# A weighted sum of gathered rows with the rows as moving operand, another order of places for the first gathers, and early scores for a second head

## The chip, the cores and the metric

The kernel runs on one core of a Trainium2 chip. The metric is the device time of one execution in microseconds. TensorE (PE) does the matrix products, VectorE (DVE), ScalarE (ACT) and GpSimd (POOL) the element-wise work; SyncE (SP) and GpSimd issue transfers, which run on sixteen DMA engines.

## The reference

Two blocks follow each other on x of 256 tokens by 1024. The change lies in the last part of the first block, the expert layer `peer_ffn`; the rest (a modulated norm, one input projection, sparse attention, a short convolution, an output projection; then two layers of window attention and spatial gating) is not touched. In short form, for each token:

```python
mod = silu(c) @ w_ada + b_ada          # six parts of 1024; gate2 is the last
h2  = rms_norm(x, norm2_w) * (1 + scale2) + shift2
q   = (h2 @ peer_wq).reshape(8 heads, 2 halves, 128)
s   = einsum(q, peer_subkeys)          # 8 heads x 2 halves x 128 keys
vals, idx = top_k(s, 16)               # in each half
top_s, pos = top_k(all 256 sums of a value of either half, 16)
expert = idx0[pos // 16] * 128 + idx1[pos % 16]
g = softmax(top_s)
a = gelu(dot(peer_u[expert], h2))      # 16 experts for each token and head
y = sum over heads and experts of g * a * peer_v[expert]
x = x + gate2 * y
```

Each of 256 tokens picks 16 experts in each of 8 heads. All is fp32.

## The kernel before

The 256 tokens are two tiles of 128, a token to a partition. A group g (0 to 15) is one head of one tile: groups 0 to 7 are the heads of tile 0, 8 to 15 those of tile 1. A group has 16 picks; pick n = 16 g + j is expert j of each of its 128 tokens. The table `peer_uv` holds a row of u and its row of v side by side, 2048 numbers or 8 KB, so one gather (GpSimd's indirect DMA at L898) brings 128 rows, 1 MB, and there are 256 gathers. They go to twelve places, six in `rows` (places 0 to 5) and six in `low_pairs` (6 to 11); pick n takes place n % 12 (`pair`, L438). All gathers stand in one queue in order, and GpSimd, which issues them in order, waits before gather n for `pair_used`, the count of picks that TensorE has summed, to show that pick n - 12 is done.

At the start some places hold something else. Places 0 to 5 lie on `flat`: places 2 and 3 are the query weights of heads 0 and 1, place 4 their keys, place 5 holds `cbc`, the silu of c in all partitions. Places 8 to 11 are `last_ada`, the eight tiles of w_ada that make gate2. Before gathers 2 and 3 GpSimd waits for TensorE's queries of head 0 and 1, before gather 4 for the scores of both, before gather 5 (`LAST_ADA_SLOT`) for all eight modulation tiles (L886 to L901).

**Routing** (`route`, L2050, on VectorE): the top 16 of each half, the top 16 of the sums, and the experts' numbers; `routed` lets GpSimd issue that group's gathers. Scores come from TensorE: `score_query(h)` makes the queries of both tiles at once (L1545), `score_keys(h)` the scores (L1558), and ACT copies both out (L1100, L1106). Head 0 of tile 0 is made ahead of that by `early_scores_of_head_0` (L1570 to L1585), so that `route(0)` starts as soon as the first tile's h2 is there. VectorE then does `route(0)`, the eight modulation tiles (`last_ada_tiles`, L1764: a product of two SBUF operands with a running sum), `route(1)`, and after that the loop over groups, in which `route(g + 2)` is cut into three parts between the dots.

**The loop over groups.** For each pick VectorE multiplies the u half of the row with h2 and sums (`dot`, L2061; h2 by token lies in PSUM). After four picks ACT makes the gelu (L1137), VectorE the weight g * a (L2068), and ACT four diagonal matrices `diag`, the identity scaled by each token's weight (L1142). TensorE then adds the v halves (`sum_pair`, L1566): for each of eight chunks of 128 columns it loads that chunk of the rows as weights and streams the diagonal matrix through, which gives the weighted rows turned, features on partitions, added up in PSUM over the 128 picks of a tile. In the profile an fp32 matmul is two records, each with a weight load of its own; so a pick is 16 records. The last group is cut finer (4, 2, 2 and then single picks), and TensorE, ACT and VectorE start the next block's first projection (`vg`) among its picks (L1609 to L1611 are its products). `join` (L2077) adds gate2 times the sum to xT, straight from PSUM. It stands after group 9 for tile 0 and at the end for tile 1; for tile 1, ACT and VectorE then split xT into a high and a low part (L1131, L2075), on which the second tile of `vg` waits.

**Order.** Each engine's order is written out by hand in its block; waits are on counting semaphores. SP loads weights in its own order; after the picks it waits for pick 253 to land before its second load of the next block, and for pick 255 before the third (L842, with L808's row loads between).

## Time and profile before

| | |
|---|---|
| median of 3 runs | 1178.29 us (1177.71 to 1179.69) |
| profiled execution | 1180.36 us |
| its span on the core | 1178.4 us, mean granted clock 0.972 |
| PE busy (matmul records) | 1051.1 us, 89%, 7587 |
| DVE busy | 837.5 us, 71% |
| ACT busy | 433.0 us, 37% |
| POOL busy | 268.8 us, 23% |
| q0, the gathers' queue | 268.45 MB, 55.0% of 16 engines |
| q1, SP's queue | 120.10 MB, 27.8% |
| q8, instructions | 60 packets, 0.98 MB, 0.3% |

All times in the profile are microseconds from the start of the span. PE is TensorE's matmuls, PEld its weight loads, which run beside them. A timeline line gives start, duration, engine, source line, operation, the tile written and those read, the shapes, the number of instructions merged into the line and, in brackets, how long the engine stood idle before and what ended that. In the views by window each engine's busy time stands with the number of instructions that ended in it, then the share of TensorE's clock that was granted, the mean busy share of the sixteen DMA engines, and GB/s.

### The profile page before, as it was taken

Reading aid. Unit: us, or ns where it says so; the run is one execution under the profiler, and the core shown is the slowest. Engines: PE = TensorE matmul, PEld = TensorE weight load, DVE = VectorE, ACT = ScalarE, POOL = GpSimd, SP = SyncE. Lnnn points to the kernel's source line nnn. Section 1 sums busy time; section 2 is a strip of 40 time slices with the busy share of each in tenths; the row PEclk is TensorE's granted clock in tenths of the full one; section 3 lists DMA queues with packets and bytes.
Section 4 is the critical chain, followed back from the end, with each engine's and each line's share of the span. In section 5 each row is a group of like instructions: output and inputs, shape, how many; then the busy total and the mean of one; then the engine's idle time right before and its main releaser. Section 6 shows DMA issues by size and latency. Waiting matters only on the chain.

```text
span 1178.4 us, 18884 instructions
## 1 busy us (share of the span) xinstructions
PE 1051.1 (89%) x7587; PEld 980.2 (83%) x7587; DVE 837.5 (71%) x1801; ACT 433.0 (37%) x913; POOL 268.8 (23%) x289
## 2 busy tenths in 40 slices
PE   8999987999999987777877778878999999999997
PEld 6999986998899877777877777778899888898886
DVE  7978889667667667666776766655756868765776
ACT  3635832123212221222122122211557654476452
POOL 1000005343334333333333333434000000300000
PEclk9999999999999999998999999989999999999999
DMA  9965988999999999999999999999854655455540
GB/s 371 406 244 180 348 313 307 420 421 420 421 420 420 421 420 421 420 421 420 420 420 421 420 421 422 420 422 420 325 208 161 237 205 184 147 211 179 186 171 36
DMA packets 59480, 390.35 MB, mean 331 GB/s; under 512 B 6785, under 2 KB 7809, under 8 KB 15618
## 3 DMA queue, kind: packets, MB, share of 16 engines
q0 software_dynamic: 36864, 268.45, 55.0%
q1 hardware_dynamic: 21056, 120.10, 27.8%
q8 instruction: 60, 0.98, 0.3%
q10 hardware_dynamic: 1474, 0.60, 0.2%
q14 instruction: 26, 0.21, 0.0%
HBM read 388.08 MB, written 1.05 MB: 330 GB/s over the span
## 4 chain that ended last, share of the span: by engine, by line
PE 63%; DMA 24%; DVE 6%; ACT 4%; issue 1%; SPq 0%; another core or an unknown queue 0%; DVEq 0%; ACTq 0%
DMA rows<-in_peer_uv,work 23%; PE aux L1566 23%; PE pj L1609 6%; PE pj L1611 5%; PE pj L1610 5%; PE aux L1545 5%; PE pj L1286 5%; PE pj L1287 4%; PE pj L1288 4%; DVE rows L2061 2%; DMA rows<-in_w_ada 1%; PE aux L1360 1%; ACT work L1142 1%; ACT rows L1010 1%; PE aux L1425 1%
## 5 line engine op out<-in xcount | busy, mean ns | idle before, releaser
L1566 PE MATMUL aux<-work,rows 128*128 128x128 f32 x2080 | 263.4, 291 | 73.8 <-ACT work L1142 73.8
L1566 PEld LDWEIGHTS aux<-work,rows 128*128 128x128 f32 x2080 | 256.2, 206 | 81.6 <-ACT work L1142 81.4
L1566 PE MATMUL aux<-work,low_pairs 128*128 128x128 f32 x2016 | 238.2, 279 | 30.2 <-ACT work L1142 30.1
L1566 PEld LDWEIGHTS aux<-work,low_pairs 128*128 128x128 f32 x2016 | 233.0, 195 | 34.0 <-ACT work L1142 34.0
L898 POOL DMA_INDIRECT rows<-in_peer_uv,work x130 | 125.5, 965 | 301.2 <-PE aux L1566 232.1
L707 DVE TENSOR_TENSOR wlo<-wring,whi 128x1024 fp32r<-128x1024 f32 x100 | 121.0, 1235 | 77.6 <-ACT whi L701 77.1
L898 POOL DMA_INDIRECT low_pairs<-in_peer_uv,work x126 | 118.3, 939 | 158.5 <-PE aux L1566 153.4
L1286 PE MATMUL pj<-xh,whi 128*128 128x256 f32 x512 | 146.3, 286 | 0.4
L1137 ACT ACTIVATE work<-work 128x4 f32<-128x4 f32 (+2 forms) x71 | 14.7, 207 | 358.3 <-DVE work L2061 358.3
L1287 PE MATMUL pj<-xl,whi 128*128 128x256 f32 x512 | 144.8, 283 | 0.0
L1288 PE MATMUL pj<-xh,wlo 128*128 128x256 f32 x512 | 144.8, 283 | 0.0
L2061 DVE CUSTOM_DVE_ANT_0 low_pairs<-low_pairs,aux 128x1024 f32<-128x1024 f32 x64 | 77.6, 1220 | 53.9 <-DMA low_pairs<-in_peer_uv,work 53.9
L701 ACT CAST whi<-wring 128x1024 fp32r<-128x1024 f32 x100 | 102.3, 1050 | 25.4 <-PE pj L1611 23.6
L2061 DVE CUSTOM_DVE_ANT_0 rows<-rows,aux 128x1024 f32<-128x1024 f32 x64 | 77.0, 1219 | 38.2 <-DMA rows<-in_peer_uv,work 38.1
L1286 PEld LDWEIGHTS pj<-xh,whi 128*128 128x128 f32 x512 | 98.1, 192 | 2.7 <-issue 1.8
L1287 PEld LDWEIGHTS pj<-xl,whi 128*128 128x128 f32 x512 | 98.2, 192 | 0.0
L1288 PEld LDWEIGHTS pj<-xh,wlo 128*128 128x128 f32 x512 | 98.2, 192 | 0.0
L2061 DVE CUSTOM_DVE_ANT_0 low_pairs<-low_pairs,pj 128x1024 f32<-128x1024 f32 x62 | 73.9, 1218 | 25.8 <-DMA low_pairs<-in_peer_uv,work 25.6
L2061 DVE CUSTOM_DVE_ANT_0 rows<-rows,pj 128x1024 f32<-128x1024 f32 x66 | 78.3, 1218 | 19.3 <-DMA rows<-in_peer_uv,work 19.0
L1142 ACT ACTIVATE work<-ident,work 128x128 f32<-128x128 f32 x256 | 82.6, 390 | 21.8 <-DVE work L2068 21.2
L1609 PE MATMUL pj<-whi,xh 128*128 128x512 f32 x192 | 75.9, 396 | 1.2 <-DVE xl L2075 1.2
L1611 PE MATMUL pj<-wlo,xh 128*128 128x512 f32 x192 | 74.8, 390 | 0.0
(288 smaller groups left out, 1461.5 us busy)
## 6 DMA issues: line engine op xcount, KB each, us to landing
wring<-in_w SPq DMA_DIRECT2D x76, 1024.0 KB, 4.8
rows<-in_w_ada SPq DMA_DIRECT2D x40, 512.0 KB, 10.1
low_pairs<-in_w_ada SPq DMA_DIRECT2D x1, 4096.0 KB, 13.4
rows<-in_w SPq DMA_DIRECT2D x3, 1024.0 KB, 10.4
rows<-in_peer_uv,work POOLq DMA_INDIRECT x130
work<-in_late_rows SPq DMA_DIRECT2D x2, 1024.0 KB, 7.5
xT<-in_gate_rows SPq DMA_DIRECT2D x2, 1024.0 KB, 7.2
rows<-in_norm_rows SPq DMA_DIRECT2D x2, 1024.0 KB, 7.3
```

Source lines behind the costliest of these rows:

```text
L701: nc.scalar.copy(layer_part("hi", l, p), layer_raw(l, p)).then_inc(w_hi, 1)
L707: dve.tensor_tensor(layer_part("lo", l, p), layer_raw(l, p), full(layer_part("hi", l, p)), ALU.subtract).then_inc(w_lo["d"], 1)
L898: pool.indirect_dma_start(out=pair(n), out_offset=None, in_=a["peer_uv"], in_offset=bass.IndirectOffsetOnAxis(ap=expert[g % EXPERTS][:, j: ...
L1142: nc.scalar.activation(diag[:, j, :], ident[:, :], ACT.Copy, scale=weight[g % 2][:, j:j + 1]).then_inc(diag_ready, 1)
L1286: mm(o, w[0], x[0], start=start, stop=False, skip_group_check=skip)
L1287: mm(o, w[0], x[1], start=False, stop=False, skip_group_check=skip)
L1288: return mm(o, w[1], x[0], start=False, stop=stop, skip_group_check=skip)
L1545: ins = mm(aux[:, 4 + s, ts], w[:, k, s * P:(s + 1) * P], hT[:, k, ts], start=(k == 0), stop=(k == KC - 1))
L1566: ins = mm(peer_sum[t][:, c * P:(c + 1) * P], pair(n)[:, D + c * P:D + (c + 1) * P], diag[:, n % PICKS, :], start=(n % (EXPERT_HEADS * PIC ...
L1609: mm(bank(u), hi[:, k, ts], w_hi_[:, j, :], start=(k == 0), stop=False)
L1611: ins = mm(bank(u), hi[:, k, ts], w_lo_[:, j, :], start=False, stop=(k == last))
L2061: v.tensor_tensor_reduce(row, row, h2_tok[g // EXPERT_HEADS], 1.0, 0.0, ALU.mult, ALU.add, dots[g % 2][:, j:j + 1]).then_inc(dotted, 1)
```

## The change

Four things are changed.

- **Rows move** (`sum_pair`): the diagonal matrix is now the loaded operand and the v half of the rows streams through, in two matmuls of 512 columns. The sums now lie by token. After the last pick of a tile, ACT copies the first half of the columns to hT (`sum_first_half_out`), VectorE the second (`sum_second_half_out`), TensorE turns both with four transposes each (`turn_sum`), and `join` reads the turned sums. For tile 0 this lies in groups 8 to 10, for tile 1 around the two last pieces of the first tile of `vg`.
- **Order of places**: pick n takes place `slot(n)`, which runs through 0, 1, 6, 7, 2, 3, 4, 8, 9, 10, 11, 5, up to pick 239; from pick 240 on the places run 0 to 11 as before. The waits of the first twelve gathers follow their places; places 8 to 11 each wait for two modulation tiles only, place 5 for all eight.
- **Early scores of head 1**: `early_scores_of` runs for heads 0 and 1 of tile 0, the second behind `turn_h2(0)`; `score_query` and `score_keys` of heads 0 and 1 then make tile 1 alone.
- **Later modulation tiles**: VectorE does `route(0)`, `route(1)` and tiles 0 and 1; tiles 2 to 5 stand behind the first four dots, 6 and 7 behind the first weights, and the bias behind the second.

```diff
@@ -46 +46 @@
 PAIRS = SLOTS - LOW_SLOTS
-AHEAD = 2
+AHEAD, EARLY_HEADS = 2, 2
@@ -265 +265 @@
 LAST_GROUP = NT * EXPERT_HEADS - 1
+FIRST_ORDER = (0, 1, 6, 7, 2, 3, 4, 8, 9, 10, 11, 5)
+LAST_ROUND = LAST_PICK // SLOTS * SLOTS - SLOTS
+def slot(n):
+    return n % SLOTS if n >= LAST_ROUND else FIRST_ORDER[n % SLOTS]
+def pick_ahead_in_slot(n):
+    return max(m for m in range(n - 2 * SLOTS, n) if m >= 0 and slot(m) == slot(n))
@@ -433 +448 @@
         LAST_ADA = 5 * KC
-        LAST_ADA_SLOT = PAIRS - 1
+        FIRST_QUERY_SLOTS, KEYS_SLOT, CONDITION_SLOT, LAST_ADA_SLOTS = (2, 3), 4, 5, tuple(PAIRS + n for n in range(2, 6))
-            k = n % SLOTS
+            k = slot(n)
@@ -887 +903 @@
                     n = g * PICKS + j
-                    if n in (2, 3):
-                        pool.wait_ge(queries, 2 * n - 2)
-                    if n == 4:
+                    k = slot(n)
+                    if n >= SLOTS:
+                        pool.wait_ge(pair_used, pick_ahead_in_slot(n) + 1)
+                    elif k in FIRST_QUERY_SLOTS:
+                        pool.wait_ge(queries, 2 * FIRST_QUERY_SLOTS.index(k) + 2)
+                    elif k == KEYS_SLOT:
                         pool.wait_ge(expert_scores, 2)
-                    if n == LAST_ADA_SLOT:
+                    elif k == CONDITION_SLOT:
                         pool.wait_ge(last_ada_used, KC)
-                    if n >= SLOTS:
-                        pool.wait_ge(pair_used, n - SLOTS + 1)
+                    elif k in LAST_ADA_SLOTS:
+                        pool.wait_ge(last_ada_used, 2 * LAST_ADA_SLOTS.index(k) + 2)
                         in_offset=bass.IndirectOffsetOnAxis(ap=expert[g % EXPERTS][:, j:j + 1], axis=0)) \
-                        .then_inc(pair_loaded[n % SLOTS], 16)
+                        .then_inc(pair_loaded[k], 16)
@@ -1102 +1121 @@
                 act.wait_ge(expert_scores, h + 1)
-                first = 1 if h == 0 else 0
+                first = 1 if h < EARLY_HEADS else 0
+            def early_head(h):
+                for s in range(2):
+                    act.wait_ge(early_query, 2 * h + s + 1)
+                    nc.scalar.copy(pq[:, h, s, 0:P], aux[:, 4 + s, 0:P]).then_inc(early_query_out, 1)
+                act.wait_ge(early_scores, h + 1)
+                nc.scalar.copy(s_all[:, h, :], aux[:, h, 0:2 * KEYS]).then_inc(early_scores_out, 1)
             shift(0)
-            for s in range(2):
-                act.wait_ge(early_query, s + 1)
-                nc.scalar.copy(pq[:, 0, s, 0:P], aux[:, 4 + s, 0:P]).then_inc(early_query_out, 1)
-            act.wait_ge(early_scores, 1)
-            nc.scalar.copy(s_all[:, 0, :], aux[:, 0, 0:2 * KEYS]).then_inc(early_scores_out, 1)
+            early_head(0)
             shift(1)
+            early_head(1)
-            for h in range(AHEAD + 1):
-                score_query(h)
-                score_out(h)
-                if h:
-                    gate_exps(h - 1)
+            score_query(0)
+            gate_exps(0)
+            score_out(0)
+            score_query(1)
+            score_out(1)
+            gate_exps(1)
+            score_query(2)
+            score_out(2)
                     nc.scalar.copy(quarter(xh, t, c), quarter(xT, t, c)).then_inc(xh_ready, 1)
+            def sum_first_half_out(t):
+                act.wait_ge(sum_first_half, t + 1)
+                nc.scalar.copy(quarter(hT, t, 0), by_chunk(peer_sum[t][:, 0:512])).then_inc(sum_out[0], 1)
@@ -1155 +1187 @@
                     gate_exps(g + AHEAD)
+                if g == EXPERT_HEADS:
+                    sum_first_half_out(0)
             layer_hi(act, 0, 2, 3)
+            sum_first_half_out(1)
@@ -1562 +1599 @@
                 pe.wait_ge(diag_ready, n + 1)
-                for c in range(KC):
-                    ins = mm(peer_sum[t][:, c * P:(c + 1) * P], pair(n)[:, D + c * P:D + (c + 1) * P], diag[:, n % PICKS, :],
-                             start=(n % (EXPERT_HEADS * PICKS) == 0 and c % 4 == 0), stop=False, skip_group_check=True)
+                of_tile = n % (EXPERT_HEADS * PICKS)
+                last = of_tile == EXPERT_HEADS * PICKS - 1
+                for c in range(2):
+                    ins = mm(peer_sum[t][:, half(c)], diag[:, n % PICKS, :], pair(n)[:, D + c * 512:D + (c + 1) * 512],
+                             start=(of_tile == 0), stop=last, skip_group_check=True)
+                    if last and c == 0:
+                        ins.then_inc(sum_first_half, 1)
-            def early_scores_of_head_0():
-                w_wait(pe, UNITS_1.index(queries_of(0)))
-                w = w_slot(UNITS_1.index(queries_of(0)))
+            def turn_sum(t, c):
+                pe.wait_ge(sum_out[c], t + 1)
+                for q in range(4):
+                    ins = nc.tensor.transpose(aux[:, 2 + c, q * P:(q + 1) * P], hT[:, 4 * c + q, tile_of(t)], ident[:, :])
+                ins.then_inc(sum_turned, 1)
+            def early_scores_of(h):
+                w_wait(pe, UNITS_1.index(queries_of(h)))
+                w = w_slot(UNITS_1.index(queries_of(h)))
                     for k in range(KC):
-                        if s == 0:
+                        if h == 0 and s == 0:
                 for s in range(2):
-                    pe.wait_ge(early_query_out, s + 1)
-                    ins = mm(aux[:, 0, s * KEYS:(s + 1) * KEYS], pq[:, 0, s, 0:P], w_slot(n)[:, 0, s * KEYS:(s + 1) * KEYS], start=True, stop=True)
+                    pe.wait_ge(early_query_out, 2 * h + s + 1)
+                    ins = mm(aux[:, h, s * KEYS:(s + 1) * KEYS], pq[:, h, s, 0:P], w_slot(n)[:, 0, (2 * h + s) * KEYS:(2 * h + s + 1) * KEYS],
+                             start=True, stop=True)
@@ -1612 +1661 @@
             keep_busy(4, 1)
-            early_scores_of_head_0()
+            early_scores_of(0)
             turn_h2(0)
+            early_scores_of(1)
             score_query(0)
-            pe.wait_ge(early_scores_out, 1)
@@ -1626 +1675 @@
                     turn_h2(1)
+                if g == EXPERT_HEADS + 2:
+                    turn_sum(0, 0)
+                    turn_sum(0, 1)
@@ -1638 +1690 @@
             pe.wait_ge(const_ready, 13)
+            pe.wait_ge(x_ready, KC)
+            turn_sum(1, 0)
@@ -1682 +1736 @@
                 if l == 0:
-                    rows_pass(l, use("vg", 0), *x_tile(l, 0), at_=(2, 3))
+                    rows_pass(l, use("vg", 0), *x_tile(l, 0), at_=(2, ))
+                    turn_sum(1, 1)
+                    rows_pass(l, use("vg", 0), *x_tile(l, 0), at_=(3, ))
@@ -1761 +1817 @@
-            def last_ada_tiles():
+            def last_ada_tiles(lo, hi):
                 dve.wait_ge(last_ada_loaded, 16)
-                for c in range(KC):
+                for c in range(lo, hi):
                                            mod[:, LAST_ADA + c:LAST_ADA + c + 1]).then_inc(last_ada_used, 1)
+            def last_ada_bias():
@@ -2018 +2076 @@
-                if g == 0:
-                    dve.wait_ge(early_scores_out, 1)
+                if g < EARLY_HEADS:
+                    dve.wait_ge(early_scores_out, g + 1)
@@ -2074 +2132 @@
+            def sum_second_half_out(t):
+                dve.wait_ge(pair_used, (t + 1) * EXPERT_HEADS * PICKS)
+                v.tensor_copy(quarter(hT, t, 1), by_chunk(peer_sum[t][:, 512:D])).then_inc(sum_out[1], 1)
                 for c in range(KC):
+                    if c % 4 == 0:
+                        dve.wait_ge(sum_turned, 2 * t + c // 4 + 1)
                     x = xT[:, c, t * P:(t + 1) * P]
-                    v.scalar_tensor_tensor(x, peer_sum[t][:, c * P:(c + 1) * P], mod[:, 5 * KC + c:5 * KC + c + 1], x, ALU.mult, ALU.add) \
+                    v.scalar_tensor_tensor(x, aux[:, 2 + c // 4, c % 4 * P:(c % 4 + 1) * P], mod[:, 5 * KC + c:5 * KC + c + 1], x, ALU.mult, ALU.add) \
-            route(0)
-            last_ada_tiles()
-            for g in range(1, AHEAD):
+            for g in range(AHEAD):
                 route(g)
+            last_ada_tiles(0, 2)
@@ -2093 +2157 @@
                         dot(g, j)
+                        if g == 0 and k == 0:
+                            last_ada_tiles(j + 2, j + 3)
                     weigh(g, k, first, size)
+                    if g == 0 and k == 0:
+                        last_ada_tiles(GROUP + 2, KC)
+                    if g == 0 and k == 1:
+                        last_ada_bias()
@@ -2113 +2183 @@
                         x0_low(0)
-                if g == EXPERT_HEADS + 1:
-                    dve.wait_ge(pair_used, EXPERT_HEADS * PICKS)
+                if g == EXPERT_HEADS:
+                    sum_second_half_out(0)
+                if g == EXPERT_HEADS + 2:
             layer_lo(dve, 0, 2, 3)
-            dve.wait_ge(pair_used, LAST_PICK + 1)
+            sum_second_half_out(1)
```

## Rows read from the trace of the kernel before

**Rows 1.** The page's slices of the span, 40 equal ones: what the transfers moved.
```profile
GB/s 371 406 244 180 348 313 307 420 421 420 421 420 420 421 420 421 420 421 420 420 420 421 420 421 422 420 422 420 325 208 161 237 205 184 147 211 179 186 171 36
```
**Rows 2.** Timeline of VectorE: dots that waited for picks 112, 231 and 247.
```profile
476.16 1.22 DVE L2061 CUSTOM_DVE_ANT_0 rows<-rows,pj 128x1024 f32<-128x1024 f32 x1 [0.77 <-DMA rows<-in_peer_uv,work]
...
776.12 1.22 DVE L2061 CUSTOM_DVE_ANT_0 rows<-rows,aux 128x1024 f32<-128x1024 f32 x1 [1.27 <-DMA rows<-in_peer_uv,work]
...
815.85 1.22 DVE L2061 CUSTOM_DVE_ANT_0 low_pairs<-low_pairs,aux 128x1024 f32<-128x1024 f32 x1 [1.25 <-DMA low_pairs<-in_peer_uv,work]
```
**Rows 3.** Windows of L2061: the dots between them, two instructions each (x).
```profile
475.90:815.80 339.90, 163.87 (x270) 0.93 1.01 421
...
776.00:815.80 39.80, 19.67 (x32) 0.91 1.01 421
```
**Rows 4.** Queues (packets, MB, share) and engines from 476 to 816; q8 also 209 to 819.
```profile
q0 software_dynamic: 19598, 142.73, 101.0%
q8 instruction: 16, 0.26, 0.3%
...
476.00:816.00 340.00, 270.94 (x2167) 264.66 (x2167) 225.80 (x545) 74.27 (x203) 125.84 (x135) 0.93 1.01 421
...
q8 instruction: 32, 0.52, 0.4%
```
**Rows 5.** Timeline around the first gathers.
```profile
171.50 0.49 DVE L2011 MAX8 work<-work 128x8 f32<-128x128 f32 x2 [1.17 <-ACT work L1114]
...
179.32 0.17 DVE L2048 SCALAR_TENSOR_TENSOR work<-work 128x16 int32<-128x16 f32 x1
...
179.41 1.22 DVE L1768 CUSTOM_DVE_ANT_0 low_pairs<-low_pairs,rows 128x1024 f32<-128x1024 f32 x1
...
179.79 1.88 POOL L898 DMA_INDIRECT rows<-in_peer_uv,work  x1 [64.82 <-DVE work L2048]
...
187.63 1.83 POOL L898 DMA_INDIRECT rows<-in_peer_uv,work  x1 [1.61 <-PE aux L1545]
```
**Rows 6.** Windows at the start: PE, PEld, DVE, ACT, POOL, clock, DMA share, GB/s.
```profile
182.30:188.00 5.70, 5.15 (x25) 4.23 (x24) 5.70 (x11) 0.74 (x2) 3.79 (x3) 1.00 1.00 356
188.00:196.00 8.00, 7.95 (x40) 6.78 (x40) 6.82 (x32) 2.64 (x5) 6.17 (x7) 1.00 0.97 330
...
206.00:240.00 34.00, 31.26 (x238) 29.89 (x236) 21.68 (x48) 5.96 (x19) 11.23 (x12) 0.97 1.01 420
```
**Rows 7.** Timeline of TensorE: transposes, 256-column records, two groups of four picks.
```profile
170.89 1.04 PE L1532 MATMUL pj<-ident,hT 128*128 128x128 f32 x8
...
180.29 7.07 PE L1545 MATMUL aux<-hT,rows 128*128 128x256 f32 x32
...
535.92 9.04 PE L1566 MATMUL aux<-work,rows 128*128 128x128 f32 x64 [2.54 <-ACT work L1142]
...
798.25 7.41 PE L1566 MATMUL aux<-work,low_pairs 128*128 128x128 f32 x64 [0.96 <-ACT work L1142]
```
**Rows 8.** Timeline of the last gathers and sums, and one window between them.
```profile
793.99 0.94 POOL L898 DMA_INDIRECT rows<-in_peer_uv,work  x1 [1.05 <-PE aux L1566]
...
817.44 0.94 POOL L898 DMA_INDIRECT rows<-in_peer_uv,work  x1 [0.85 <-PE aux L1566]
...
824.00:832.00 8.00, 7.73 (x67) 7.35 (x66) 5.55 (x12) 3.89 (x10) 0.68 (x1) 1.00 0.72 281
...
836.88 0.80 SPq L842 DMA_DIRECT2D wring<-in_w  x2
...
841.80 1.95 PE L1566 MATMUL aux<-work,rows 128*128 128x128 f32 x16
...
843.79 2.16 DVE L2080 SCALAR_TENSOR_TENSOR xT<-aux,mod,xT 128x128 f32<-128x128 f32 x8 [0.92 <-PE aux L1566]
...
844.95 0.62 ACT L1131 CAST xh<-xT 128x512 fp32r<-128x512 f32 x1 [3.52 <-DVE xT L2080]
...
846.69 0.47 PE L1609 MATMUL pj<-whi,xh 128*128 128x512 f32 x1 [0.21 <-DVE xl L2075]
```

15 lines of the change are left out of this document (9 added, 6 removed).

## The prediction

> **What bounds the kernel now.** I read the page's slices first: from about 206 to 825 us the transfers run flat at 420 to 422 GB/s [rows 1], so this half of the span is set by the gathers of 256 MB (256 picks of 128 rows of 8 KB) and by what else shares the transfer engines. What can move the time is when that stretch begins, how evenly it runs, and what follows it.
>
> Then the waits of VectorE, which takes the picks in order. Its dots wait for a DMA; picks 231 and 247 were taken at 776.12 and 815.85, 16 picks in 39.73 us, 2.483 us a pick [rows 2, 3]. That is the pace of an undisturbed queue (8 KB x 128 / 422 GB/s). But from 476.16 (pick 112) to 815.85 there are 135 picks (270 instructions, two for a dot) in 339.69 us, 2.516 us a pick [rows 2, 3]: landings slip by 339.69 - 135 x 2.483 = 4.5 us against their own undisturbed pace, although the queue never ran dry. The gathers moved 142.73 MB between 476 and 816, 136.1 picks [rows 4]; VectorE could take 135. A pick has landed only when all sixteen engines have brought their part, so the slowest engine fell over a pick behind the mean. The end of the stage shows the same: all gathers are issued by 817.44, yet between 824 and 832 the engines are busy for only 0.72 of the time, and the SP load that waits for the last pick goes out at 836.88 [rows 8]. Most engines are done while a few bring the last picks.
>
> What holds these few up? The only other traffic between 476 and 816 is the instruction queues [rows 4]. q8 brings 16 packets of 16 KB, 0.26 MB, and TensorE ran 2167 matmul and 2167 weight-load records in that time: 60 bytes a record. So q8 is TensorE's program. Its packets took 0.3% of sixteen engines' 340 us, about 1.0 us of one engine each.
>
> **The change part by part.**
>
> *First gathers.* The first route ends at 179.32 + 0.17 and the first gather is issued at 179.79. From then on VectorE runs the eight modulation tiles (two operands in SBUF, 1.22 us), GpSimd needs 1.88 us for an issue where the last one took 0.94 [rows 5, 8], and the third to fifth gathers wait for TensorE's weight places: the fourth goes out at 187.63. The queue runs thin: 356 GB/s from 182.3 to 188 and 330 to 196, against 420 after 206 [rows 6]. Lost: 5.7 x (1 - 356/420) + 8 x (1 - 330/420) = 2.6 us. After the change picks 0 to 3 go to places that nothing holds, and VectorE is in route(1) instead of the tiles, so issues should come every 0.94 + 0.3 us: four by 184, seven by about 188. Of the 2.6 us I take back 2.1 (the first pick still ramps up), and 0.9 us from the faster first issue: -3.0. Bounds: -3.5, and +2 if picks 7 to 11 come late, since they now wait for modulation tiles that stand between VectorE's first dots. That wait is covered: route(1) takes 8.0 us as route(0) did (171.50 to 179.49 [rows 5]), tiles 0 and 1 end near 190, tile 7 near 203; seven picks issued by 188 feed the queue until 182 + 7 x 2.48 = 199, each later tile pair frees a pick some 3 us before its turn, and one 1 MB weight load lies between. GpSimd is in order, so a late tile would hold all gathers behind it; that is the +2.
>
> *Early scores of head 1* move 32 records of 128 columns ahead of score_query(0), and halve those of score_query(1): nothing net on TensorE, which waits there anyway. They let route(1) follow route(0) at once. 0.
>
> *Rows moving.* A pick is 8 matmuls of 128 columns now: 64 records for 4 picks in 7.41 us, 16 records or 1.85 us a pick. A 256-column fp32 record takes 7.07/32 = 0.221 us [rows 7], so 4 records of 512 take 4 x 0.442 = 1.77. With 2.483 us a pick on the queue, TensorE's 0.08 us is worth nothing inside the stage.
>
> Its program is another matter. 256 x 16 records become 256 x 4, matmul and weight load each: 6144 fewer x 64 bytes = 0.39 MB, 24 of the 32 packets that q8 brings between 209 and 819 [rows 4]. If bytes alone counted, that gives back 0.39 MB / 421 GB/s = 0.9 us. By the slip it is more: 16 packets went with 4.5 us, 0.28 us each on the engine that ends last; 24 x 0.28 = 6.7 us. I take -5.5, below that because few packets fall less evenly on sixteen engines than many. Bounds -6.7 and -0.9.
>
> Against this reading: the trace shows a slow engine, and the Trainium skill (DMA: Bandwidth & Descriptors, "Latency and other measured facts") says that two of the sixteen engines are usually slower under software-made descriptors, with the fetches of these descriptors as its best guess. By that rule the slow engine stays as slow, and the sum would have -0.9 here in place of -5.5. The trace speaks for single events rather than a slow engine: 16 picks on end keep 2.483 us [rows 2, 3], which a steadily slower engine would not better over 40 us and lose over 340.
>
> *Order of places at the end.* From pick 240 places run 0 to 11 again. Place 5 was last taken by pick 239, so gather 245, and all behind it, wait for the sum of 239 (before: of 233; issued at 793.99). That sum ends at about 798.25 + 7.1 = 805.3, and 245 lands at 815.85 - 2 x 2.483 = 810.9, so the slow engine must have it by 808.4 [rows 2, 7, 8]. From issue to first bytes takes some 2 us (179.79 to 182.3): covered by about 1 us, not if TensorE's clock dips just there, which costs 9.04 - 7.41 = 1.6 us [rows 7]. I take +0.3; bounds 0 and +2.
>
> *The end of the sum.* Sums now lie by token and must be turned. Before: the last pick's matmuls end at 841.80 + 1.95 = 843.75, eight joins take 2.16, the ACT copy 0.62 beside them, and TensorE starts the second tile of the first projection at 846.69, 2.94 after the sum; in between it runs 12 products in at most 0.245 us each [rows 8]. After: ACT copies the first half (0.62) beside the second half's matmuls (0.88), four transposes take 4 x 1.04/8 = 0.52 [rows 7], six products 1.4, four transposes 0.52, four joins 1.08, the low part 0.7: with semaphores about 4.5 after the sum, +1.6. The sixteen picks of the last head, where TensorE works off a backlog, win 0.08 each, a little over 1.0 in all with the products between them. Net +0.6, bounds -1.0 and +2. For tile 0 the same work lies in the middle of the stage, where picks queue for some 16 us: 0. What is late next is the first projection, on whose end the rest hangs, so these sums carry through.
>
> **Sum**: -3.0 - 5.5 + 0.3 + 0.6 = -7.6 us. The profiled execution has a span of 1178.4 and took 1180.36; the median of the runs is 1178.29. The difference of 2 us lies outside of the span and I apply the sum to the median: **1170.7 us**.
>
> **Rivals.**
> *The slip stays* (the engine is slow for another reason, or a few packets still meet the same engine): -3.0 - 0.9 + 0.9 = -3.0, 1175.3. For it: nothing in a row names the engines. Against it: the single events above.
> *The first gathers gain nothing* because places freed by tiles come too late, and the switch of order drains the queue: 0 + 2 - 5.5 + 0.6 = -2.9, 1175.4. For it: seven picks of lead at the start, one microsecond at the end; against it, the counts above.
> *TensorE's clock makes it the bound* (slower): a group of four picks takes 4 x 1.77 = 7.1 us at the full clock of the two levels (2.4 GHz) and the queue needs 9.93, so idle per group grows from 2.5 to 2.8 us. After such an idle time (2.54) one group already ran partly at 1.2 GHz and took 9.04 [rows 7]. It decides when the mean granted clock falls below 7.1/9.93 = 0.71; at 0.65 a group takes 10.9, 64 groups lose 64 x 1.0, and the time is about 1235. Against it: the mean was 0.93 over 476 to 816 [rows 4], and a dip makes the next idle shorter. The Trainium skill (TensorE: Matmul & The Clock Gate, "Why this matters for your kernels") warns of just this, bursts with waits between them that each start at the low clock; the trace agrees that it happens, at a price that the 2.8 us hide.
>
> **How the numbers follow.** Forecast 0.62, with its own range 1168 to 1173.5 (slip -4 to -6.7, the others near their values). The slip stays 0.18; nothing at the start 0.10; slower by the clock or a like stall 0.06; still faster than all this 0.04. The first two rivals lie just beyond 0.2% (2.4 us, about what can be told from no change), so part of each counts as no change: faster 0.62 + 0.12 + 0.05 + 0.04 = 0.83, same 0.11, slower 0.06. Range for 8 in 10: 1167 to 1176.
>
> **What would show it.** First route: gathers 1 to 4 issued within 5 us of 179.8, and 420 GB/s from about 184 on. q8: 8 or 9 packets in place of 32 through the stage. The slip: VectorE's waits at nearly 2.483 us a pick over hundreds of picks, and a load that waits for the last pick within some 14 us of the last gather's issue (19.4 before). Tail: the second tile of the projection 4.5 us after the sum. The prediction is wrong if landings keep 2.516 with q8 cut, if VectorE's early dots wait for gathers 7 to 11, or if transfers sag near pick 245.

## The result: 1.9 us slower, not 7.6 us faster

| | before | after |
|---|---|---|
| median, range (18 runs each, same chip) | 1179.37 us (1177.71 to 1182.07) | 1180.72 us (1178.82 to 1183.57) |
| ratio after / before | | 1.0016, 95% interval 1.0009 to 1.0022 |
| profiled execution, span | 1180.36 us, 1178.4 us | 1180.40 us, 1178.4 us |

By the ratio that is +1.9 us (1.1 to 2.6); the medians differ by 1.35. The prediction said -7.6 and left 0.06 for slower. The two profiled executions happen to take the same time, which is the first warning: one execution of each does not show a difference of 2 us. So two more of before and one more of after were profiled, and all five are cut at the same events: the first gather's issue, VectorE taking pick 27 and pick 231 (both waiting for a DMA), the SP load that waits for pick 255, the second tile of the first projection, the end of the span. Lengths in us, each a difference of two timeline rows:

```
                first issue   to pick 27   27 to 231   to the load   to tile 2   to the end
before             179.79       79.66       516.67       60.76         9.81       331.7
before, second     181.38       77.95       515.98       60.85         8.31       331.6
before, third      181.30       78.22       516.01       60.77         8.31       331.8
after              181.54       77.02       516.24       62.38         9.23       332.0
after, second      180.10       76.80       516.74       63.48         9.98       332.1
means, change        0.00       -1.70       +0.27        +2.14        +0.80       +0.35
```

The sum is +1.86 us, within the measured interval. That it meets 1.9 so closely is luck: it comes from three and two executions, whose spans run from 1176.1 to 1179.2 us. The first gathers do gain, the long middle gains nothing, and the end loses more than the start won.

**The profile after.** The page: engine rows, slices of GB/s, and the queue of TensorE's program.

```profile
PE 1043.3 (89%) x4563; PEld 700.4 (59%) x4563; DVE 838.0 (71%) x1803; ACT 434.6 (37%) x918; POOL 267.3 (23%) x289
...
GB/s 373 406 225 196 338 301 339 422 422 421 420 421 422 421 421 422 421 422 421 422 421 421 422 420 422 420 400 335 401 201 168 230 210 179 149 210 179 187 170 36
...
q8 instruction: 36, 0.59, 0.2%
```

Matmul records fell from 7587 to 4563, and the middle is as flat as before; new are the 400 and 335 in slices 27 and 28, where [rows 1] has 422 and 420, and the 401 in slice 29 (325 there), where what was held up is made good. Then the queues between 209 and 819 us (packets, MB, share):

```profile
q0 software_dynamic: 34662, 252.45, 99.8%
q1 hardware_dynamic: 144, 1.05, 0.4%
q8 instruction: 9, 0.15, 0.1%
q14 instruction: 15, 0.12, 0.0%
```

q8 went from 32 packets to 9, as forecast [rows 4]. q14, with 14 packets and a share of 0.0% in the kernel before, does not occur in the prediction. VectorE's takes of picks 27 and 231 in after:

```profile
258.56 1.22 DVE L2119 CUSTOM_DVE_ANT_0 low_pairs<-low_pairs,pj 128x1024 f32<-128x1024 f32 x1 [1.25 <-DMA low_pairs<-in_peer_uv,work]
...
774.80 1.22 DVE L2119 CUSTOM_DVE_ANT_0 low_pairs<-low_pairs,aux 128x1024 f32<-128x1024 f32 x1 [1.26 <-DMA low_pairs<-in_peer_uv,work]
```

and in the second execution of before:

```profile
259.33 1.22 DVE L2061 CUSTOM_DVE_ANT_0 rows<-rows,pj 128x1024 f32<-128x1024 f32 x1 [0.49 <-DMA rows<-in_peer_uv,work]
...
775.31 1.22 DVE L2061 CUSTOM_DVE_ANT_0 rows<-rows,aux 128x1024 f32<-128x1024 f32 x1 [1.25 <-DMA rows<-in_peer_uv,work]
```

516.24 and 515.98 us for the same 204 picks: 2.531 and 2.529 us a pick, where an undisturbed queue gives 2.483. The slip that was to go is all there.

### The profile page after: what moved, and what is told of

It reads as the page before. It is cut to its first block, busy times and chain, and to the rows that moved or that the text cites. A ratio compares the mean times of both kernels' runs of the same rounds, so it can differ in the third digit from the quotient of the medians.

```text
span 1178.4 us, 12844 instructions
## 1 busy us (share of the span) xinstructions
PE 1043.3 (89%) x4563; PEld 700.4 (59%) x4563; DVE 838.0 (71%) x1803; ACT 434.6 (37%) x918; POOL 267.3 (23%) x289
## 4 chain that ended last, share of the span: by engine, by line
PE 55%; DMA 30%; DVE 8%; ACT 4%; issue 2%; SPq 1%; POOL 0%; DVEq 0%
DMA low_pairs<-in_peer_uv,work 25%; PE aux L1605 17%; PE pj L1658 5%; PE pj L1660 5%; PE pj L1659 5%; PE pj L1321 5%; PE pj L1322 4%; PE pj L1323 4%; PE aux L1580 4%; DMA rows<-in_w_ada 2%; DMA rows<-in_peer_uv,work 2%; DVE low_pairs L2119 2%; ACT work L1174 1%; ACT rows L1029 1%; PE aux L1460 1%
## 5 line engine op out<-in xcount | busy, mean ns | idle before, releaser
L1605 PE MATMUL aux<-rows,work 128*128 128x512 f32 x520 | 263.2, 654 | 83.9 <-ACT work L1174 83.9
L1605 PE MATMUL aux<-low_pairs,work 128*128 128x512 f32 x504 | 232.5, 606 | 28.5 <-ACT work L1174 28.5
L1605 PEld LDWEIGHTS aux<-rows,work 128*128 128x128 f32 x520 | 104.8, 208 | 232.6 <-issue 120.7
L917 POOL DMA_INDIRECT rows<-in_peer_uv,work x130 | 123.1, 947 | 308.6 <-PE aux L1605 237.1
L1605 PEld LDWEIGHTS aux<-low_pairs,work 128*128 128x128 f32 x504 | 95.9, 193 | 156.1 <-issue 113.4
L723 DVE TENSOR_TENSOR wlo<-wring,whi 128x1024 fp32r<-128x1024 f32 x100 | 121.0, 1235 | 77.6 <-ACT whi L717 77.1
## 6 DMA issues: line engine op xcount, KB each, us to landing
rows<-in_w_ada SPq DMA_DIRECT2D x40, 512.0 KB, 10.1
```

Source lines behind the costliest of these rows:

```text
L723: dve.tensor_tensor(layer_part("lo", l, p), layer_raw(l, p), full(layer_part("hi", l, p)), ALU.subtract).then_inc(w_lo["d"], 1)
L917: pool.indirect_dma_start(out=pair(n), out_offset=None, in_=a["peer_uv"], in_offset=bass.IndirectOffsetOnAxis(ap=expert[g % EXPERTS][:, j: ...
L1605: ins = mm(peer_sum[t][:, half(c)], diag[:, n % PICKS, :], pair(n)[:, D + c * 512:D + (c + 1) * 512], start=(of_tile == 0), stop=last, ski ...
```

## The experiments

Ratios are to before on the same chip, with 95% intervals.

**Executions again.** Before twice more, after once more, unchanged (the table above).

> The kernel before, unchanged, for a second profiled execution. Its first one had no half-clock stretch near 70 us and took 1180.36 us, over its median of 1179.4; the changed kernel's had one and took 1180.40 us, its median. Theory: the stretch comes and goes from execution to execution of every kernel (its first 170 us are the same code), so that the two profiles can't be compared before the first gather. Then a second profile shows another moment of the clock's first rise (10.4 us in the first one) and, if it rises near 11 to 13 us, the half clock near 69 to 71 and a first gather at 181.5. Rival: it belongs to the kernel; then again 10.4 us, no half clock at 70 and 179.8.

> The kernel before, unchanged, a third profiled execution. In its first one: 42.4 us from the first gather's issue to the landing of pick 12, 576.3 to that of pick 240, 38.4 to that of pick 255, 9.8 to the second tile of the projection, 331.7 to the end. Theory: these repeat within 0.5 us. Rival: the first profile of the kernel before was slower in the gathers than usual (its time lay 1 us over the median), and the usual one lands pick 255 a microsecond or two sooner.

> The changed kernel, unchanged, for a second profiled execution. From the first gather's issue on the first profile gives 39.7 us to the landing of pick 12, 575.8 to that of pick 240, 40.1 to that of pick 255, 9.2 to the second tile of the projection and 332.0 to the end. Theory: these repeat within 0.5 us, and only what lies ahead of the first gather differs. Rival: one of them differs by 1 us or more, and the profile that I explain was not a usual one.

The first profile of before differs from the two others in two terms: its first gathers took 1.6 us longer and its tail 1.5 us. The first goes with its first gather, issued 1.6 us earlier than theirs: pick 27 was taken at nearly the same moment in all three (259.45, 259.33 and 259.52 us).

**One part at a time.** rows_only is before with nothing but the moved rows and the turned sums. rows_still is after with the old sum:

```diff
-for c in range(2):
-    ins = mm(peer_sum[t][:, half(c)], diag[:, n % PICKS, :], pair(n)[:, D + c * 512:D + (c + 1) * 512],
...
+for c in range(KC):
+    ins = mm(peer_sum[t][:, c * P:(c + 1) * P], pair(n)[:, D + c * P:D + (c + 1) * P], diag[:, n % PICKS, :],
```

order_kept is after with the switch of order put off from pick 240 to pick 252 (`LOW_PICKS`):

```diff
-return n % SLOTS if n >= LAST_ROUND else FIRST_ORDER[n % SLOTS]
+return n % SLOTS if n >= LOW_PICKS else FIRST_ORDER[n % SLOTS]
```

> The kernel before with only the sums changed: rows moving, the sums turned at the end. Places, first gathers, scores and modulation tiles as before. My theory: -0.4 us in the landings and -0.6 us after the last pick, about 1178.4 us (ratio 0.999) and 8 or 9 instruction packets of 16 KB in the stage, with the engine that lands last still 9 to 10 us behind the first at pick 240. Rival, as recorded in the prediction: the program fetches were the slip, then 1173.5 us and a spread of 4 to 5 us. Rival on the other side: moving rows cost, then 1181 us.

> The changed kernel with the rows as loaded operand again (sum_pair, join and the turning as before); the first gathers, early scores, later tiles and the order of places stay. My theory: moving rows is worth 0.4 us in the landing of the picks (two thirds of TensorE's program fetches gone, but none of them on the engine that lands last) and 0.6 us after the last pick, so this kernel takes 1 us more than the changed one, about 1181.7 us, and its 16 KB instruction packets are 32 again between 209 and 819. Rival: the moving rows cost something, in TensorE's clock or at the reads of the rows, that eats the gain of the first gathers; then this kernel is faster than the changed one, 1179 us or less. My recorded prediction would have it 5 us slower.

> The changed kernel with one edit: the first order of the places is kept up to pick 251, and only the last four picks take places 0 to 3. So no gather waits for a pick that is less than ten ahead. My theory: the switch at pick 240 let gather 245 wait until 804.27 for the sum of pick 239, the queue ran dry on fifteen engines (378 and 273 GB/s in two windows), and the last picks land some 1.6 us later for it. Expected: 420 GB/s from 780 to 825, pick 255 lands 1.5 us earlier after pick 240 than in the changed kernel (38.5 us instead of 40.1), and a time 1.6 us below the changed kernel, about 1179.1 us (0.0% against the kernel before). Rival: the engine that lands last had work enough all through the sag, so that it costs nothing; then 1180.7 us.

rows_only: 1179.93 us, 1.0004 (0.9995 to 1.0013). Its q8 brings 10 packets, and 27 to 231 takes 515.64 us: with the program cut and nothing else touched, the slip stays. rows_still: 1182.67 us, 1.0025 (1.0014 to 1.0035); its program is as long as before (32 packets of q8), and 27 to 231 takes 516.70; what it loses, it loses at the end, 64.3 us from pick 231 to the load. So the slip does not follow the length of TensorE's program.

order_kept: 1181.47 us, 1.0027 (1.0016 to 1.0037). The sag at the end is gone. Its windows (length; busy us and count of PE, PEld, DVE, ACT, POOL; clock, DMA share, GB/s):

```profile
780.00:800.00 20.00, 15.89 (x33) 6.56 (x32) 10.35 (x19) 2.97 (x10) 7.91 (x9) 0.91 1.01 420
800.00:816.00 16.00, 13.21 (x28) 5.50 (x27) 8.82 (x15) 2.38 (x8) 5.24 (x6) 0.89 1.01 421
```

against the same windows of after:

```profile
780.00:800.00 20.00, 16.12 (x34) 6.52 (x33) 10.22 (x20) 2.97 (x10) 4.46 (x5) 0.91 0.96 378
800.00:816.00 16.00, 12.96 (x27) 5.42 (x26) 7.71 (x14) 2.38 (x8) 8.99 (x10) 0.89 0.72 273
```

Pick 255 landed in time (the load goes out 60.52 us behind pick 231; in after it was 62.38). But the time did not fall, for another wait took the place of the one removed. Timeline of order_kept, its tail:

```profile
819.81 0.94 POOL L917 DMA_INDIRECT rows<-in_peer_uv,work  x1 [0.78 <-PE aux L1605]
820.76 0.36 POOL L922 IOTA rstd<- 128x256 int32 x1
821.15 1.71 DVE L2177 TENSOR_SCALAR work<-rstd 128x256 f32<-128x256 int32 x8 [4.43 <-POOL rstd L922]
...
849.11 0.47 PE L1658 MATMUL pj<-whi,xh 128*128 128x512 f32 x1 [0.51 <-DVE xl L2133]
```

The last gather now waits for the sum of pick 245 and is issued 3.1 us later than in after (816.70). Behind it on GpSimd stands an iota for a bias, and VectorE, which is in order, stood 4.43 us for that iota before it could take its last picks.

**Which program it is.** q14 was the suspect, and VectorE's program the candidate: between two q14 packets of 8 KB that matter VectorE runs 105 to 135 recorded instructions, 61 to 78 bytes for each. (The Trainium skill, Perfetto Trace Analysis, "Per-instruction lifecycle: what the profiler-reported window actually captures", gives 64 bytes an instruction; the trace agrees, as 64 lies in that range.) dve_pad gives VectorE 912 more small instructions, four after each dot of picks 12 to 239, and leaves the rest. route_once takes instructions away: `route_halves` and `route_pairs` return at once and `route_experts` keeps only its last instruction, so that groups 2 to 15 gather the rows of the second head again; the number of gathers, dots and sums stays, and so does the undisturbed pace (picks 26 and 27 are taken 2.48 us apart). The cuts of the two edits, dve_pad first:

```diff
+if SLOTS <= n < LAST_ROUND:
+    for i in range(4):
+        v.memset(pad[32 * i:32 * i + 32, n:n + 1], 0.0)
```
```diff
+if g >= EARLY_HEADS:
+    return
```

> The changed kernel with four more tiny VectorE instructions (memsets of one column on 32 partitions) behind each dot of picks 12 to 239: 912 instructions, 58 KB of program, about 7 packets of 8 KB more on the instruction queue q14. Nothing waits for them and VectorE has idle time. My theory: the steps by which the last engine falls behind come with the 8 KB packets of VectorE's program (seven steps of 1.0 us at 350.8, 416.4, 489.2, 558.8, 630.1, 698.4 and 762.8, a packet at each), so there will be some seven steps more, the spread between the first and the last engine at pick 240 grows from 9.2 to about 16 us, and the time by about 7 us, to 1187.7 us. Rival 1: that engine is slow by itself or through the gathers' descriptors: no change, 1180.7 us, spread 9.2. Rival 2: the packets at the steps are GpSimd's program (29 gathers between two steps): the number of packets grows but not the steps, 1180.7 us.

> The changed kernel without the routing of groups 2 to 15: of each such group only the last instruction of route_experts is left, so that these groups gather the experts of the second head again (the result is another one; the gathers, dots and sums are as many as before). About 434 VectorE instructions fewer, 28 KB of program, 3.4 packets of 8 KB. My theory (the engine that lands last is held 1 us by each fetch of VectorE's program): the 8 KB packets between 209 and 819 fall from 15 to 11 or 12, the spread at pick 240 from 9.2 to about 5.8 us, and the time by 3.4 us to about 1177.3 us, though VectorE was never what was waited for. Rival: that engine is slow by itself, and only an overload made it worse in dve_pad; then 9.2 us and 1180.7 us.

Queues of dve_pad between 209 and 819 us:

```profile
q8 instruction: 9, 0.15, 0.1%
q14 instruction: 22, 0.18, 0.1%
```

and of route_once:

```profile
q8 instruction: 9, 0.15, 0.1%
q14 instruction: 11, 0.09, 0.0%
```

The takes of pick 231, dve_pad first (pick 27 at 259.99), then route_once (pick 27 at 258.18):

```profile
781.37 1.22 DVE L2120 CUSTOM_DVE_ANT_0 low_pairs<-low_pairs,aux 128x1024 f32<-128x1024 f32 x1 [0.94 <-DMA low_pairs<-in_peer_uv,work]
```
```profile
770.87 1.22 DVE L2124 CUSTOM_DVE_ANT_0 low_pairs<-low_pairs,aux 128x1024 f32<-128x1024 f32 x1 [1.25 <-DMA low_pairs<-in_peer_uv,work]
```

q8 is the same in both; q14 goes 11, 15, 22 and 27 to 231 goes 512.69, 516.24, 521.38 us: 8.7 us for 11 packets, 0.8 us a packet, although a packet itself takes 0.32 us. Not all of q14 is VectorE's program: five packets stand at nearly the same times in all three kernels (225.1, 278.4, 436.8, 544.6 and 617.7 in after), however many instructions VectorE has. Without these, 4, 8 and 13 packets come between picks 27 and 231, and in dve_pad pick 27 had landed 0.8 us before VectorE took it; by landings it is 9.5 us for 9 packets, 1.06 us each. In time: dve_pad 1187.86 us, 1.0070 (1.0055 to 1.0086); route_once 1177.67 us, 0.9986 (0.9976 to 0.9995), where 1.0016 is after. In dve_pad VectorE still waits for a DMA at pick 231, so it is not VectorE's own added work that sets the pace there.

The trace also has the moments at which the sixteen parts of a gather report, without the names of the engines. Their lag, last part behind first, in after and dve_pad, at gathers where it grows (of those with all sixteen reports), beside the q14 packet just ahead:

```
after    packet at  350.8  416.4  489.2  558.8  630.1  698.4  762.8
         landed at  353.8  419.4  492.5  560.6  633.7  701.7  764.8
         lag        2.30   3.23   4.26   5.31   6.31   7.30   8.23   before the step
                    3.09   4.21   5.23   6.27   7.29   8.25   9.17   behind it
dve_pad  packet at  250.9  290.1  329.9  366.3  441.5  482.0  522.5  554.8
         landed at  254.2  295.0  333.2  369.0  443.0  483.8  524.5  557.8
         lag        1.85   2.62   3.60   4.63   6.60   7.64   8.65   9.64   before the step
                    2.54   3.57   4.57   5.59   7.61   8.63   9.63   10.62  behind it
```

dve_pad has six more, at 405.2 (5.61 to 6.60) and, of 0.9 to 1.0 us each, at 595.2, 635.6, 667.5, 706.0 and 746.0; between these its lag shrinks, because the first part comes later too. In after, from 416.4 on, only the last of the sixteen parts moves at a step: one engine loses about 1.0 us with each such packet and keeps the loss. At the five packets that are not VectorE's the last part doesn't move. In before there are five steps between 476 and 816 (packets at 490.9, 560.2, 620.5, 699.8, 764.1), and the lag grows from 5.66 to 10.1: 4.45 us, the slip of 4.5 that the prediction had read from VectorE's takes. The two other executions of before have such steps behind the same packets.

**Repairing the end.** kept_early is order_kept with the iota ahead of group 14's gathers and the bias tiles that use it one group earlier; rows_early does the same to rows_only.

```diff
 for g in range(NT * EXPERT_HEADS):
+    if g == LAST_GROUP - 1:
+        pool.iota(distance, ...).then_inc(bias_iota, 1)
...
-elif g == NT * EXPERT_HEADS - 1 and k == 2:
+elif g == LAST_GROUP - 1 and k == 2:
```

> order_kept (the first order of places up to pick 251) with one more edit: GpSimd writes the distances (its iota) ahead of the gathers of group 14 and no longer behind the last gather, and VectorE makes the eight bias tiles from them in group 14 and no longer between the dots of the last group. My theory: order_kept lost its gain because the last gather now waits for the sum of pick 245, the iota stands behind it on GpSimd, and VectorE stood 4.43 us before the iota's result with dots already landed behind it. Expected: no wait of VectorE for GpSimd near 821, the last dot at once when pick 255 lands (about 835.7), the second tile of the projection 9.2 us after that, 845 instead of 849.1 us, and a time some 4 us below order_kept, 1177.5 to 1178 us (ratio 0.999). Rival: order_kept is slow for its places themselves; then it stays at 1181.5 us.

> rows_only (the kernel before with rows moving and turned sums alone) with the early iota and bias tiles of kept_early. In rows_only the second tile of the projection began 10.4 us after the last pick had landed, in the changed kernel 9.2. My theory: the difference is VectorE's wait for the iota and the 1.7 us of bias tiles between the last dots, so that here it is 9.2 us again and the time 1.2 us below rows_only, about 1178.7 us (ratio 0.9995). Rival: the tail is bound by what TensorE has queued; then nothing changes, 1179.9 us.

kept_early: 1180.98 us, 1.0011 (1.0002 to 1.0020). Its tail:

```profile
835.66 0.80 SPq L858 DMA_DIRECT2D wring<-in_w  x2
...
844.94 0.47 PE L1659 MATMUL pj<-whi,xh 128*128 128x512 f32 x1 [0.51 <-DVE xl L2134]
```

From the load to the second tile 9.28 us where order_kept took 13.36: the 4.1 us came back in this execution. By the ratios it is only 1.9 us (0.16% of 1179); the stall on the iota need not be as long in every execution, and that was not followed up. rows_early: 1181.72 us, 1.0020 (1.0011 to 1.0029), against 1.0004 for rows_only, which is not what was expected: its profile shows no loss from the load to tile 2 (9.33, rows_only 10.40). Why its runs are slower stays open.

**A stretch of half clock.** Near 70 us, long before the gathers, TensorE ran at the lower of its two levels in 10 of the 13 profiles of kernels with no filler there. Timeline of TensorE in after:

```profile
66.79 1.84 PE L1437 MATMUL aux<-blk,low_pairs 128*128 128x2 f32 x16
69.65 0.36 PE L1321 MATMUL pj<-whi,xh 128*128 128x256 f32 x1 [1.01 <-DVE wlo L657]
```

and its windows (columns as above):

```profile
70.00:72.00 2.00, 2.00 (x13) 2.00 (x12) 2.00 (x8) 0.25 (x2) 0.00 (x0) 0.57 0.72 168
72.00:74.00 2.00, 2.00 (x13) 2.00 (x12) 1.87 (x5) 0.00 (x0) 0.00 (x0) 0.58 0.84 356
```

Sixteen products of two columns and 1.01 us of idle time, then a granted clock of 0.57 (1.00 before it). The same two stand in the first profile of before, where the clock stays at 1.00. The code is the same before and after the change, and the stretch comes and goes: the three profiles without it issue the first gather at 179.79 to 180.26, nine of the ten with it at 181.24 to 181.68 (the tenth, kept_early_fill below, has more to do before it). Eight products of 128 columns were added, first behind the second sums of q and k, past the gap (kept_early_fill), then behind the first ones, in the gap (kept_early_fill2), and also in before and with the rows as the loaded operand again:

```diff
 qk_sums(0)
+for _ in range(8):
+    mm(aux[:, 5, 0:P], ident[:, :], ident[:, :], start=True, stop=True)
 token_major(h_in)
```

> kept_early with eight products of 128 columns (identity by identity, into a bank that nobody reads) behind the second sums of q and k, where TensorE stands idle for 1.0 us before 69.65. In the profile of the changed kernel, and of three kernels made from it, the granted clock was at half from 70.3 to 73.7, right behind this idle time, and the first gather was issued 1.75 us later; in the kernel before and in rows_only it was not. Theory: this loss comes in most executions of the changed kernel; then the clock stays at 1.00 there and the time falls by 1.75 us against kept_early, to about 1176 us. Rival: it falls on some executions of every kernel alike; then the medians differ by 0.9 us or less. Second rival: the idle time is not what the clock answers to; then 0.57 to 0.72 is granted there again and nothing changes.

> kept_early with the eight products of 128 columns behind the first sums of q and k, where the idle time of 1.0 us stands (in kept_early_fill they stood behind the second ones, 20 us later, and the idle time was as before). Theory: the half clock at 70 us answers to this stretch, 1.8 us of products of two columns and 1.0 us of idle time; filled, the clock stays at 1.00 there in the profile, and since the stretch came in 8 of 10 profiles the median falls by 0.8 x 1.75 = 1.4 us against kept_early, to 1179.6 us. Rival: the eight products are too little, 0.5 to 0.6 granted again, no change.

> The kernel before with the eight products behind the first sums of q and k alone. The half clock near 70 us came in two of the three profiles of the kernel before. Theory: filled, it comes no more, and the median falls by 0.7 x 1.75 = 1.2 us, ratio 0.999. Rival: it is worth less here than in the changed kernel; ratio 1.000. With still_kept_early_fill2 it also says what first gathers, kept order and early bias are worth without rows moving: theory 1 us.

> kept_early_fill2 with the rows as loaded operand again (sum_pair and join as before, no turning), so that rows moving is the only difference between the two, without the stall at pick 245 and without the wait for the iota. From the profiles: the turning puts the second tile of the projection 4.27 us after the last sum and not 3.07 (1.2 us), the stretch from there to the end is 332.0 us with it and 331.7 without (0.3 us), and a pick's sum takes 1.88 and not 1.95 us. Theory: rows moving costs 1.2 + 0.3 - 0.1 = 1.4 us, and nothing in the landings; then this kernel is 1.4 us faster than kept_early_fill2, about 1178 us, ratio 0.999 or a little less, and the second tile begins 8.3 us after the last landing. Rival: the shorter sums win the turning back, since TensorE works off a backlog of single picks; then no difference, ratio 1.000. My recorded prediction has the other sign: 6 us slower without moving rows.

kept_early_fill: 1.0016 (1.0005 to 1.0026); the idle time ahead of 69.46 remained, and so did the half clock, so it says nothing of the gap. kept_early_fill2, the gap filled:

```profile
68.25 2.03 PE L1443 MATMUL aux<-ident 128*128 128x128 f32 x16
```
```profile
70.00:72.00 2.00, 2.00 (x19) 2.00 (x18) 2.00 (x6) 0.00 (x1) 0.00 (x0) 1.00 0.83 217
72.00:74.00 2.00, 2.00 (x19) 2.00 (x18) 1.62 (x4) 0.00 (x0) 0.00 (x0) 1.00 0.73 307
```

Clock 1.00, 1179.9 us, 1.0000 (0.9990 to 1.0009): 1.3 us less than kept_early by the ratios, whose intervals overlap. The half clock near 70 us is in none of the three profiles with the gap filled; three are few. In before the filler gave 0.9996 (0.9987 to 1.0006), which is no measurable gain; its profile has a dip at 134.6 us in place of this one, and in before an earlier first gather did not land pick 27 any earlier (above). still_kept_early_fill2: 1177.61 us, 0.9991 (0.9981 to 1.0000), the lowest of the kernels that do all the work, but not apart from before by more than the measurement can tell. Against kept_early_fill2, moving the rows would cost 1.1 us, but these intervals overlap too, and rows_still against after (1.0025 and 1.0016) points the other way. What moving the rows costs or gives by itself is open; rows_only against before bounds it at -0.6 to +1.5 us.

## Why the prediction was wrong, step by step

**The step that failed: "I take -5.5" for the slip.** The prediction saw the right loss (an engine over a pick behind, 4.5 us between picks 112 and 247) and put it on q8, the one queue of a program that it looked at. q8 went to 9 packets and the loss stayed: 516.2 to 516.7 us in after, 515.6 in rows_only. What holds the last engine are VectorE's program packets, which the change does not thin out (1801 instructions before, 1803 after): about 1.0 us for each, by the steps and by dve_pad and route_once. Cutting q8 did help the engines that don't count: at about pick 240 the lags of the sixteen add up to 36 us in place of 64 to 70, while the last is 9.2 to 9.4 us behind the first, as in before (10.1, 8.8 and 8.9 in its three executions). Placing the slip in time would have told q8 from q14: q8's 16 packets come every 20 us or so, while the five steps are 60 to 80 us apart, each behind a packet of q14. The prediction read only the sum of the slip, at its two ends. Two of its own signs of being wrong came: landings kept their slow pace with q8 cut, and the transfers sagged near pick 245. The rival *the slip stays* (0.18) had this step right. The Trainium skill's rule behind it (DMA: Bandwidth & Descriptors, "Latency and other measured facts"), that two engines are usually slower, agrees with the trace only in that an engine ends late: here it is one, and it falls behind in steps, with the fetches of VectorE's program.

**First gathers: -3.0, measured -1.9** (mean 77.05 us to pick 27 in nine profiles with the new first order, 78.9 in six with the old one; dve_pad is left out, since its pick 27 waited for VectorE). The issues came as forecast, four within 5 us. Timeline of GpSimd in after:

```profile
181.54 1.17 POOL L917 DMA_INDIRECT rows<-in_peer_uv,work  x1 [64.83 <-DVE work L2106]
183.01 0.94 POOL L917 DMA_INDIRECT rows<-in_peer_uv,work  x1 [0.30 <-issue]
...
185.50 0.94 POOL L917 DMA_INDIRECT low_pairs<-in_peer_uv,work  x1 [0.31 <-issue]
...
201.09 0.94 POOL L917 DMA_INDIRECT low_pairs<-in_peer_uv,work  x1 [3.64 <-DVE mod L1824]
```

The feared holds by modulation tiles came (3.00, 3.64 and 3.04 us) and cost nothing, as the cover was there; the windows stay full:

```profile
184.05:189.75 5.70, 2.83 (x26) 2.67 (x25) 5.39 (x16) 0.53 (x2) 3.50 (x4) 1.00 0.96 387
189.75:197.75 8.00, 8.00 (x32) 6.75 (x31) 7.96 (x16) 1.04 (x4) 4.09 (x4) 0.79 1.02 430
```

The size was off because the loss was read from one execution, and misread: the 356 and 330 GB/s of [rows 6] came with a DMA share of 1.00 and 0.97, so the engines were busy and slow, not short of work. The second execution of before has more at the same place:

```profile
183.90:189.60 5.70, 5.15 (x25) 4.23 (x24) 5.70 (x11) 0.74 (x2) 3.78 (x3) 1.00 1.00 369
189.60:197.60 8.00, 7.94 (x40) 6.77 (x40) 6.81 (x32) 2.64 (x5) 6.17 (x7) 1.00 1.00 396
```

By the prediction's formula that is 5.7 x (1 - 369/420) + 8 x (1 - 396/420) = 1.1 us lost, not 2.6. The first issue became 0.7 us shorter (1.17 for 1.88), forecast 0.9. The old order also had a loss that no earlier issue mends: there pick 27 came at 259.3 to 259.5 us whether the first gather went out at 179.8 or at 181.3, while with the new order it follows the issue (258.56 for 181.54, 256.90 for 180.10). What held the old order back was not tried.

**Order of places at the end: +0.3, measured +2.1** (60.8 to 62.4 and 63.5 us). The wait that the prediction counted came when it said, gather 245 behind the sum of 239 at a computed 805.3. It missed an earlier one: with the switch, gathers 242 to 244 take the places of picks 232 to 234, ten picks back and not twelve, so gather 242 already waits for the sum of pick 232. In order_kept it is issued at 783.14, in after at 790.92, and from 790 to 795 us the queue moves 293 GB/s. Gathers 242 and 245:

```profile
790.92 0.94 POOL L917 DMA_INDIRECT rows<-in_peer_uv,work  x1 [8.96 <-PE aux L1605]
...
804.27 0.94 POOL L917 DMA_INDIRECT rows<-in_peer_uv,work  x1 [8.98 <-PE aux L1605]
```

The cover was counted for the engine that ends last. The fifteen others had nothing left, so the rate fell to 378 and then 273 GB/s (windows above), and by their reports gathers 245, 246 and 247 landed 0.3, 1.2 and 1.6 us behind their pace (the 0.3 stood already at 241). The sixteen parts of 245 landed within 0.6 us of each other: the lead of the fifteen, some 9 us, was gone. That is the prediction's bound of +2, taken as an outside case; order_kept shows that it is the switch.

**Early scores and rows moving inside the stage: 0, and 0 it was** (first issue at the same mean, 27 to 231 +0.27).

**End of the sum: +0.6, measured +0.8** (9.8, 8.3 and 8.3 us from the load to tile 2 in before, 9.2 and 10.0 in after, so that +0.8 is no better than a microsecond). After's last sum and its turning:

```profile
840.26 1.88 PE L1605 MATMUL aux<-rows,work 128*128 128x512 f32 x4
841.32 0.59 ACT L1163 COPY hT<-aux 128x512 f32<-128x512 f32 x1
842.05 0.63 PE L1615 MATMUL aux<-ident,hT 128*128 128x128 f32 x4
...
844.54 1.13 DVE L2145 SCALAR_TENSOR_TENSOR xT<-aux,mod,xT 128x128 f32<-128x128 f32 x4 [0.22 <-PE aux L1615]
...
846.41 0.47 PE L1658 MATMUL pj<-whi,xh 128*128 128x512 f32 x1 [0.52 <-DVE xl L2133]
```

The sum ends at 842.14 and tile 2 starts 4.27 us later (2.94 in [rows 8]), forecast 4.5. The backlog that was to give back 1.0 us did not show: a pick's sum went from 1.95 to 1.88 us, as forecast, but it is landings and VectorE's chain that set the last picks. A further 0.3 us in the last stage, in kernels with both moved rows and new order, has no cause yet.

**TensorE's clock as the bound (1235)** did not come: granted 0.90 to 0.97 from 400 to 800 us.

**The sum again**, by the five profiles of the table: -1.7 + 0.3 + 2.1 + 0.8 + 0.35 = +1.9. Of the 9.5 us between forecast and result, 5.8 are the slip, 1.8 the order at the end and 1.3 the first gathers.

## What to carry to other kernels

When one transfer engine ends last, place its losses in time before naming their cause: steps can be matched with packets, a total can't, and a queue with 0.0% of the share can own every step. Count cover against all engines of a queue, not only the slowest: a wait that the slowest absorbs still drains the others. And before resting 2 us on a window, look at the same window in a second execution, and at the share beside the GB/s.

## What was not expected of the hardware

- A program packet of 8 KB for VectorE takes 0.32 us by its record and puts its engine about 1.0 us behind, which it keeps while the queue stays full (why three times its own length, and why on one engine, was not tried); q8's packets of 16 KB, 1.07 us each by their records, cost the landings nothing that could be measured.
- TensorE's clock fell to its lower level near 70 us in 10 of 13 executions, of kernels with the same code up to there; a first issue after it came some 1.4 us later.
- Gathers moved 366 to 396 GB/s in two executions and 330 to 356 in a third at the same place with the engines' share at 0.96 or more; what slowed them was not tried.
